# A hybrid convolution decoder layer: the token-row loads go out from SP's DMA queue in place of GpSimd's

## Chip, cores and metric

One Trainium2 chip, all 8 cores. Each core runs the same program on its own share of the tokens, and no core talks to another. The time is that of the slowest core in device microseconds, as the median of several executions.

## What is computed

The layer takes a prompt of 8 x 2048 tokens and 128 x 8 sample tokens, all 1024 wide. Each core gets one prompt sequence and 16 sample sequences of 8 tokens: 2176 token rows. Cut to what matters here:

```
u    = rmsnorm(h, g_mix);  proj = u @ w_in                      # 1024 -> 9 * 1024
ya   = (a_b * dwconv3(a_c * a_h) * silu(a_z)) @ w_out_a         # short convolution
yb   = (silu(layernorm(dwconv31(b_v * sigmoid(b_g)) + bias)) * silu(b_z)) @ w_out_b
m    = sigmoid(gate_a) * ya + sigmoid(gate_b) * yb
h    = h + m @ w_o
h    = h + sigmoid(rmsnorm(h, g_ple) @ w_pg) * (p @ w_pe)
y    = rmsnorm(h, g_final)
```

## The kernel before

A core's 2176 rows are done in two blocks, one after the other: block 0 with 1152 rows (9 tiles of 128), block 1 with 1024 (8 tiles). Each block goes through the same stages. Stages 2 to 5 work with channels on the partitions: projections (`mm8`, L581), the two convolutions, the layer norm, the gated output projections. Their weights come through a ring of 14 tiles, loaded from GpSimd's queue (L393) as TensorE frees them. The last part of stage 5 is the loop over `BORDER`, eight calls of `s5_b`, in which the weights of the next stage are fetched too: `wpg_stage` (L515) loads rows of `w_pg` from SP's queue, `wpg_scale` (L519) scales them on ScalarE.

Stage 6 then goes through the block's tiles with tokens on the partitions. For tile t:

- `s6_A` (L1000): 16 matmuls, m @ w_o. `s6_Aev` (L1011, VectorE) adds the token rows `xs`, ScalarE copies the sum as bf16 into `xb` (L1015), and SP issues a DMA transpose of `xb` into `u2T` (L1019). The first and the last tile are transposed on TensorE instead (`s6_B`, L1028, copied by L1032).
- `s6_C`: 4 matmuls with `pT` (L1044), then 16 with `u2T` (L1052), then a tanh on ScalarE (L1066).
- `s6_E` and `s6_D` (L1074, L1089, VectorE) join the two and scale by the final norm; SP stores the tile to `y` (L1093).

TensorE takes A(t+1) before C(t), and `u2T` of tile t+1 is asked for right after A(t+1) is evicted, so a transpose has about the time of C(t) and of A(t+2) and the `pT` matmuls to land.

While block 0 is in stage 6, the first steps of block 1 are done beside it: for each of block 1's 8 tiles ScalarE squares the token rows (`s1_stats`), VectorE scales them into `xn` (`s1_scale`, L544), and SP issues a DMA transpose into `uT` (`s1_xbar`, L550). So each step of stage 6 of block 0 reads two tiles of x: its own one again, for the residual, and one of the next block. In block 1 there is only the own one.

These 25 reads of x share four buffers `xs0` to `xs3`, in the order of the list `XU` (n0, n1, o0, o1, n2, o2, n3, o3, ...: n of the next block, o of the own one). `xload` (L455) issues one read of 512 KB, `xdone` asks for the next as soon as a buffer is free, that is, after the VectorE instruction that read it last. The first four reads are asked for in the `BORDER` loop of block 0, one in each of its last four rounds (`xload(i - 3)`, L1249). All 25 are issued by GpSimd, in its program order, between the ring loads and the small steps of the row norms (L416, L421).

The first nine tiles of x, at the kernel's start, are loaded apart from that by `x0load` (L483) from SP's queue; the ninth takes buffer `xs0` again and signals on a semaphore of its own, `x0e`.

`Sched` makes a list of all operations in the order of the Python program. An engine takes its own ones in this order and waits before each until what it depends on is done. A wait therefore holds up everything behind it on that engine. SP's order for one step t of stage 6 in block 0 is: transpose u2T(t+1), store y(t-1), transpose uT(t+1).

Of the kernel before, what the change touches and what calls it, by code (L numbers as in the profile page):

```python
# [167 lines left out]
def build_program():  # L168
    nc = bass.Bass("TRN2", target_bir_lowering=False)

    def din(name, shape):
        return nc.dram_tensor(name, shape, F32, kind="ExternalInput").ap()
# [4 lines left out]
    x_d = din("x", [NTOK, D])  # L177
# [27 lines left out]
    with contextlib.ExitStack() as st:  # L205
        def sb(name, shape, dt):
            return st.enter_context(nc.sbuf_tensor("t_" + name, shape, dt))
# [38 lines left out]
        NXS = 4  # L246
        xs = [sb(f"xs{i}", [128, D], F32) for i in range(NXS)]
# [21 lines left out]
        S = Sched(nc)  # L269
# [165 lines left out]
        def tiles_of(b):  # L435
            blk = BLOCKS[b]
            n = (2 * NP // blk["pb"]) * blk["wb"] // 128
            return [blk["row0"] + 128 * i for i in range(n)]

        XU = []  # L440
# [9 lines left out]
        def xload(upto):  # L450
            while xst["nl"] < min(upto, len(XU)):
                u = xst["nl"]
                xst["nl"] += 1
                k = u % NXS
                S.add("pool", lambda e, k=k, r=XU[u]: e.dma_start(out=xs[k][:], in_=x_d[r:r + 128, :]),  # L455
                      writes=[f"xs{k}"], dma=f"xs{k}")

        def xuse(row0):
# [5 lines left out]
        def xdone(u):  # L464
            xst["done"].add(u)
            while xst["nd"] in xst["done"]:
                xst["nd"] += 1
            xload(xst["nd"] + NXS)
# [4 lines left out]
        x0 = []  # L473
        xw = [t.rearrange("p (h m) -> p h m", h=2) for t in xs]
        for i, r in enumerate(tiles_of(0)):
            t, nm = (xw[i], f"xs{i}") if i < NXS else (AB[i - NXS], ("A0", "A1", "B0", "B1")[i - NXS]) \
# [3 lines left out]
        def x0load(i):  # L480
            t, nm = x0[i]
            r = tiles_of(0)[i]
            S.add("sp", lambda e: e.dma_start(out=t, in_=x_d[r:r + 128, :].rearrange("t (h m) -> t h m", h=2)),  # L483
                  writes=[nm], dma=f"x0{nm}" if i < NXS + 4 else "x0e")

        x0load(0)
        S.add("sp", lambda e: e.dma_start(out=vecs[:], in_=vecs_d), writes=["vecs"], dma="vecs")
        for i in range(1, NXS + 4):
            x0load(i)
# [3 lines left out]
        for i in range(2):  # L493
# [6 lines left out]
              writes=["ssq63"])  # L500
# [62 lines left out]
        def do_block(bi, blk):  # L563
# [577 lines left out]
            if bi == 0:  # L1141
# [18 lines left out]
                pump(1)  # L1160
                sc(0)
                x0load(NXS + 4)
                fill(20)
                turn(0, 4)
# [82 lines left out]
            for i, j in enumerate(BORDER):  # L1247
                s5_b(j)
                if bi == 0 and i >= 4:  # L1249
                    xload(i - 3)  # L1250
                if i == 0:
                    wpg_stage(0)
                    wpg_stage(1)
                    if nxt:
                        S.add("sp", lambda e: e.dma_start(out=gmix, in_=gmix_d), writes=["gmix"], dma="gmix")
                if bi == 1 and i == 2:
                    S.add("sp", lambda e: e.dma_start(
                        out=hist_d[:, 0:480], in_=sb_d.rearrange("c s w -> c (s w)")), dma="hist")
                if i == 6 and nxt:
                    s1_scale(*s1_stats(nxt[0]), 0)  # L1260
                if i == 7 and nxt:
                    pre[1] = s1_stats(nxt[1])
                if 2 <= i <= 5:
                    for k in (2 * i - 4, 2 * i - 3):
                        wpg_scale(k)
                        if k + 2 < NCH:
                            wpg_stage(k + 2)
                if i == 5:
                    last_weights("wpe", [0, 1])
                if i == 5:  # L1270
                    S.add("pool", lambda e, r0=blk["row0"]: e.dma_start(
                        out=pT[:, :, 0:N], in_=pT_d[:, :, r0:r0 + N].rearrange("q p t -> p q t")),
                        writes=["pT"], dma="pT")
                    if last:

                        S.add("pool", lambda e: e.drain())
# [139 lines left out]
```

How the kernel before makes its waits and increments, by code:

```python
            def run(engname, e):  # L123
                waited = {}
                for o in ops:
                    if o["eng"] != engname:
                        continue
                    need = {}
                    for d in o["deps"]:
                        od = ops[d]
                        v = od["seq"] * (16 if od["dma"] is not None else 1)
                        if v > need.get(od["chan"], 0):
                            need[od["chan"]] = v
                    for c, v in need.items():
                        if waited.get(c, 0) >= v:
                            continue
                        e.wait_ge(sems[c], v)
                        waited[c] = v
                    ins = o["fn"](e)
                    if o["signal"]:
                        ins.then_inc(sems[o["chan"]], 16 if o["dma"] is not None else 1)
                if engname == final_wait_eng:
                    for c, v in final.items():
                        if waited.get(c, 0) < v:
                            e.wait_ge(sems[c], v)
```

## Time and profile before

| | |
|---|---|
| median of 3 runs | 886.32 us (882.65 to 887.99) |
| the profiled execution | 886.32 us |
| its span on the slowest core, core 3 | 884.6 us |
| spans of all cores | 863.0 to 884.6 us |
| TensorE busy in that span | 852.0 us, 96% |
| VectorE, ScalarE, GpSimd | 476.7, 305.9, 225.2 us |
| DMA queue 0 (GpSimd's) | 70.83 MB |
| DMA queue 1 (SP's) | 61.29 MB |

The profile shows one execution, on the core whose span was longest. Times in the rows are counted from that core's first instruction. PEclk is the granted TensorE clock as a share of 2.4 GHz. The DMA share is the mean busy share of 16 DMA engines as their packets' times add up, and it can exceed 1 where packets of two queues overlap on an engine. "Landing" is the time from the issue of a DMA to its semaphore.

### The profile page before, as it was taken

The page shows a single profiled execution, that of the slowest core. Times are in us where ns is not written, and L with a number is a line of the kernel's source. Part 1 is how long each engine was busy: PE and PEld are TensorE (multiplying, and loading weights), DVE is VectorE, ACT ScalarE, POOL GpSimd, SP SyncE. Part 2 cuts the span into 40 slices and gives each one's busy share as a digit, 9 for nine tenths or more (in the row PEclk, how much of TensorE's full clock was granted, in tenths as well). Part 3 has the DMA queues.
Part 4 walks back from the last instruction along what each step waited for, and adds up shares of the span by engine and source line. Part 5 has one row for each costly group of instructions (what it writes and reads, how often), then busy time and mean ns, then how long its engine had stood idle before and what let it go on. Part 6 is the DMA issues. An engine that isn't in the chain of part 4 may idle for free.

```text
span 884.6 us, 16617 instructions; the slowest of 8 cores (863.0 to 884.6 us)
## 1 busy us (share of the span) xinstructions
PE 852.0 (96%) x5790; PEld 501.6 (57%) x5790; DVE 476.7 (54%) x672; ACT 305.9 (35%) x430; POOL 225.2 (25%) x427
## 2 busy tenths in 40 slices
PE   8899999999999999999869999999999999999995
PEld 3677777777777777773324444444444444444442
DVE  4545566776848622344646344555567374234565
ACT  4212232232345522435635212222224343142554
POOL 4432333333112211133533222222221121000221
PEclk9999999999999999999989999999999999999998
DMA  8999999999959754997997698999998798342542
GB/s 237 154 173 195 211 159 159 168 159 168 159 105 183 112 86 67 203 169 194 199 194 222 134 164 122 138 136 154 141 138 123 177 197 128 51 150 41 148 114 103
DMA packets 88825, 133.43 MB, mean 151 GB/s; under 512 B 37272, under 2 KB 45736, under 8 KB 86696
## 3 DMA queue, kind: packets, MB, share of 16 engines
q0 software_dynamic: 36992, 70.83, 48.9%
q1 hardware_dynamic: 51608, 61.29, 34.3%
q8 instruction: 47, 0.77, 0.4%
q14 instruction: 34, 0.28, 0.1%
q10 hardware_dynamic: 144, 0.26, 0.1%
HBM read 169.26 MB, written 17.25 MB: 211 GB/s over the span
## 4 chain that ended last, share of the span: by engine, by line
PE 83%; DMA 7%; DVE 3%; issue 2%; ACT 2%; SPq 1%; POOL 0%; DVEq 0%; POOLq 0%; ACTq 0%
PE ps L581 70%; DMA t_xs<-x 5%; PE ps L1052 5%; PE ps L1000 4%; PE ps L719 3%; DMA t_u2T<-t_xb 2%; PE ps L1044 1%; ACT t_tmp L413 1%; SPq L483 1%; DVE t_cbuf L1011 1%; DVE t_tmp L860 0%; SPq L490 0%; DVE t_uT L558 0%; ACT t_xb L1015 0%; DVE t_tmp L863 0%
## 5 line engine op out<-in xcount | busy, mean ns | idle before, releaser
L581 PE MATMUL ps<-t_uT,t_ring 128*128 128x288 bf16 (+1 forms) x3456 | 545.1, 319 | 2.8 <-DVE t_uT L558 2.4
L581 PEld LDWEIGHTS ps<-t_uT,t_ring 128*128 128x128 bf16 x3456 | 338.0, 98 | 202.7 <-issue 15.7
L393 POOL DMA_DIRECT2D t_ring<-w_in x144 | 78.5, 546 | 302.9 <-PE ps L581 281.0
L1052 PE MATMUL ps<-t_reg,t_u2T 128*128 128x512 bf16 x272 | 66.1, 399 | 13.5 <-DMA t_u2T<-t_xb 11.5
L937 ACT ACTIVATE t_tmp<-ps 128x576 f32<-128x576 f32 (+1 forms) x48 | 36.7, 772 | 113.6 <-PE ps L581 113.6
L945 DVE SCALAR_TENSOR_TENSOR t_tmp<-t_tmp,ps 128x576 f32<-128x576 f32 (+1 forms) x27 | 24.6, 910 | 85.8 <-PE ps L581 85.8
L581 PE MATMUL ps<-t_yaT,t_ring 128*128 128x288 bf16 (+1 forms) x384 | 63.9, 325 | 0.0
L581 PE MATMUL ps<-t_cbuf,t_ring 128*128 128x288 bf16 (+1 forms) x384 | 61.6, 317 | 0.0
L1000 PE MATMUL ps<-t_cbuf,t_yaT 128*128 128x512 bf16 x272 | 61.6, 381 | 0.0
L1052 PEld LDWEIGHTS ps<-t_reg,t_u2T 128*128 128x128 bf16 x272 | 27.2, 102 | 50.8 <-issue 23.1
L904 DVE TENSOR_TENSOR t_tmp<-ps,t_tmp 128x576 f32<-128x576 f32 (+1 forms) x24 | 21.8, 912 | 60.1 <-PE ps L581 60.1
L643 DVE SCALAR_TENSOR_TENSOR t_vta<-t_tmp,ps 128x512 bf16<-128x512 f32 (+1 forms) x24 | 20.7, 863 | 60.4 <-ACT t_tmp L640 52.9
L413 ACT ACTIVATE t_tmp<-t_cbuf 128x1024 bf16<-128x1024 f32 x37 | 38.8, 1050 | 39.4 <-DVE t_cbuf L1077 33.1
L581 PEld LDWEIGHTS ps<-t_yaT,t_ring 128*128 128x128 bf16 x384 | 38.2, 100 | 22.9 <-issue 3.4
L640 ACT ACTIVATE t_tmp<-ps 128x576 f32<-128x576 f32 (+1 forms) x24 | 18.6, 775 | 91.5 <-PE ps L581 91.5
L581 PEld LDWEIGHTS ps<-t_cbuf,t_ring 128*128 128x128 bf16 x384 | 37.6, 98 | 21.4
L1000 PEld LDWEIGHTS ps<-t_cbuf,t_yaT 128*128 128x128 bf16 x272 | 26.6, 98 | 32.2 <-issue 1.2
L416 POOL TENSOR_SCALAR t_msq<-t_ssq 128x1 f32<-128x1 f32 x50 | 14.1, 283 | 115.0 <-ACT t_tmp L413 114.7
L902 ACT ACTIVATE t_tmp<-ps 128x576 f32<-128x576 f32 (+1 forms) x24 | 18.6, 775 | 69.5 <-PE ps L581 69.5
L1074 DVE SCALAR_TENSOR_TENSOR t_cbuf<-t_cbuf,ps 128x1024 f32<-128x1024 f32 x16 | 19.5, 1220 | 39.5 <-ACT t_cbuf L1066 39.5
L890 ACT ACTIVATE t_tmp<-ps 128x576 f32<-128x576 f32 (+1 forms) x24 | 18.6, 775 | 58.9 <-PE ps L581 53.2
L421 POOL TENSOR_TENSOR t_rsd<-t_msq,t_mhalf 128x1 f32<-128x1 f32 x50 | 32.0, 641 | 7.7 <-POOL t_msq L416 0.4
(115 smaller groups left out, 815.4 us busy)
## 6 DMA issues: line engine op xcount, KB each, us to landing
t_ring<-w_in POOLq DMA_DIRECT2D x144, 256.0 KB, 6.8
t_xs<-x POOLq DMA_DIRECT2D x25, 512.0 KB, 7.9
y<-t_cbuf SPq DMA_DIRECT2D x16, 512.0 KB, 4.3
t_reg<-vd SPq DMA_DIRECT2D x32, 132.0 KB, 6.0
t_reg<-vd SPq DMA_DIRECT2D x32, 131.9 KB, 6.4
t_reg<-vd SPq DMA_DIRECT2D x32, 131.9 KB, 7.5
t_reg<-vd SPq DMA_DIRECT2D x32, 131.9 KB, 8.2
t_ring<-w_cv POOLq DMA_DIRECT2D x16, 256.0 KB, 9.1
```

The lines of the kernel that those rows point to most:

```text
L393: S.add("pool", lambda e, k=k, src=src: e.dma_start(out=ring[k][:, :], in_=src), writes=[f"ring{k}"], dma=f"ring{k}")
L413: S.add("act", lambda e, c=c: e.activation(out=junk.rearrange("p (h m) -> p h m", h=2), in_=src_ap, func=AF.Square, accum_out=ssq[:, c:c + ...
L421: S.add("pool", lambda e, c=c: e.tensor_tensor(out=rsd[:, c:c + 1], in0=msq[:, c:c + 1], in1=mhalf[:, 0:1], op=ALU.pow), reads=[f"msq{c}", ...
L581: S.add("pe", lambda e, k=k, si=si, c0=c0: e.matmul(ps[:, b + si, 0:wb], lhsT=ring[k_][:, 128 * k:128 * k + 128], rhs=src[:, k, c0:c0 + wb ...
L643: S.add("dve", lambda e, bv=bv, tg=tg, u=u: e.scalar_tensor_tensor(out=pph(vt[v], u), in0=pcols(two(tg)), scalar=1.0, in1=pcols(pp(bv)), o ...
L719: S.add("pe", lambda e, b=b, r=r, i=i, g=g, wc=wc, rhs=src[:, c0:c0 + w], w=w: e.matmul(ps[32 * g:32 * g + 32, b + r, 0:w], lhsT=ring[kc][ ...
L904: S.add("dve", lambda e: e.tensor_tensor(out=two(tz), in0=pp(bb), in1=two(tz), op=ALU.mult), reads=pres(bb) + [tzr], writes=[tzr])
L937: S.add("act", lambda e: e.activation(out=two(tg), in_=pp(bg), func=AF.Tanh, scale=0.5), reads=pres(bg), writes=[tgr])
L945: S.add("dve", lambda e: e.scalar_tensor_tensor(out=dst.rearrange("p (s n) -> p s n", s=2), in0=two(tg), scalar=1.0, in1=pp(b), op0=ALU.ad ...
L1000: S.add("pe", lambda e, h=h, k=k: e.matmul(ps[:, b + h, :], lhsT=yaT[:, k, 128 * ti:128 * ti + 128], rhs=wo_t[:, k, 512 * h:512 * h + 512] ...
L1052: S.add("pe", lambda e, h=h, k=k: e.matmul(ps[:, bg + h, :], lhsT=u2Ts[sl][:, k, :], rhs=wpg_t[:, k, 512 * h:512 * h + 512], start=(k == 0 ...
L1074: S.add("dve", lambda e: e.scalar_tensor_tensor(out=B2, in0=B2, scalar=1.0, in1=ps[:, be:be + 2, :], op0=ALU.add, op1=ALU.mult), reads=pre ...
```

## The change

The reads of x by `xload` are issued by SP in place of GpSimd, all 25 of them, at the same places of the program. The ninth tile of the start, which was on SP already, signals on the semaphore of buffer `xs0` in place of one of its own. Sizes, buffers and the conditions under which a read may go out stay as they are.

```diff
@@ -452,7 +452,7 @@
                 u = xst["nl"]
                 xst["nl"] += 1
                 k = u % NXS
-                S.add("pool", lambda e, k=k, r=XU[u]: e.dma_start(out=xs[k][:], in_=x_d[r:r + 128, :]),
+                S.add("sp", lambda e, k=k, r=XU[u]: e.dma_start(out=xs[k][:], in_=x_d[r:r + 128, :]),
                       writes=[f"xs{k}"], dma=f"xs{k}")
@@ -481,7 +481,7 @@
             S.add("sp", lambda e: e.dma_start(out=t, in_=x_d[r:r + 128, :].rearrange("t (h m) -> t h m", h=2)),
-                  writes=[nm], dma=f"x0{nm}" if i < NXS + 4 else "x0e")
+                  writes=[nm], dma=f"x0{nm}" if i < NXS + 4 else "xs0")
```

SP's order for one step t of stage 6 in block 0 becomes: u2T(t+1), y(t-1), x, x, uT(t+1); in block 1: x, u2T(t+1), y(t-1).

## Rows read from the trace of the kernel before

**Rows 1.** Spans and mean granted clock of two of the eight cores.

```profile
core 3: 884.6 us, clock 0.982
core 6: 863.0 us, clock 0.997
```

**Rows 2.** Windows, core 3: busy PE, PEld, DVE, ACT, POOL; PEclk, DMA share, GB/s.

```profile
395.00:487.00 92.00, 77.72 (x345) 33.73 (x343) 50.18 (x44) 46.35 (x71) 34.05 (x63) 0.94 0.98 202
820.00:840.00 20.00, 20.00 (x95) 9.04 (x94) 10.61 (x9) 11.17 (x16) 5.23 (x13) 1.00 0.54 134
844.00:860.00 16.00, 16.00 (x76) 7.21 (x74) 10.06 (x9) 9.12 (x14) 3.09 (x9) 1.00 0.35 99
```

**Rows 3.** Windows, core 6, the same columns: its stage 6 of block 0.

```profile
391.00:469.00 78.00, 72.81 (x345) 32.46 (x344) 50.37 (x44) 46.58 (x71) 37.80 (x65) 1.00 1.08 234
```

**Rows 4.** Timeline of PE, core 3: start, us; in brackets idle before and releaser.

```profile
395.25 7.07 PE L1000 MATMUL ps<-t_cbuf,t_yaT 128*128 128x512 bf16 x32
...
406.10 5.05 PE L1052 MATMUL ps<-t_reg,t_u2T 128*128 128x512 bf16 x16
...
445.74 5.30 PE L1052 MATMUL ps<-t_reg,t_u2T 128*128 128x512 bf16 x16 [4.54 <-DMA t_u2T<-t_xb]
...
460.68 5.07 PE L1052 MATMUL ps<-t_reg,t_u2T 128*128 128x512 bf16 x16 [5.33 <-DMA t_u2T<-t_xb]
...
483.48 3.61 PE L1052 MATMUL ps<-t_reg,t_u2T 128*128 128x512 bf16 x16 [0.87 <-ACT t_u2T L1032]
486.93 3.40 PE L581 MATMUL ps<-t_uT,t_ring 128*128 128x512 bf16 x15
```

**Rows 5.** Waits, core 3, 395 to 487 us: total, times, longest.

```profile
PE ps L1052 <- DMA t_u2T<-t_xb: 11.5, 3, 5.3
```

**Rows 6.** Chain that ended last, core 3: start, us, what.

```profile
388.64 12.70 DMA t_xs<-x
401.43 0.70 DVE t_cbuf L1011
...
429.68 12.35 DMA t_xs<-x
...
444.62 15.79 DMA t_u2T<-t_xb
...
842.31 3.45 PE ps L1052 x16
...
850.08 3.45 PE ps L1052 x16
```

**Rows 7.** Timeline of POOL, core 3, 387 to 430 us.

```profile
388.12 0.53 POOL L393 DMA_DIRECT2D t_ring<-w_in  x1 [3.30 <-PE ps L581]
...
420.85 1.13 POOL L455 DMA_DIRECT2D t_xs<-x  x2
```

**Rows 8.** Timeline of SP, core 3: start of issue, us it took.

```profile
371.22 0.33 SPq L515 DMA_DIRECT2D t_xb<-w_pg  x1
...
419.99 0.66 SPq L1093 DMA_DIRECT2D y<-t_cbuf  x1
420.75 1.83 SPq L550 DMA_TRANSPOSE t_uT<-t_xn  x1
426.11 1.29 SPq L1019 DMA_TRANSPOSE t_u2T<-t_xb  x1
...
450.76 8.17 SPq L550 DMA_TRANSPOSE t_uT<-t_xn  x1
...
844.48 1.23 SPq L1019 DMA_TRANSPOSE t_u2T<-t_xb  x1
```

**Rows 9.** Landing of u2T (L1019), core 3: 400 to 480, then 840 to 870 us.

```profile
DMA to landing us min/median/max: 3.1/7.0/15.8
DMA to landing us min/median/max: 3.1/3.1/3.1
```

**Rows 10.** Landing of the x reads (L455), core 3, 400 to 480 us.

```profile
DMA to landing us min/median/max: 5.5/9.0/14.7
```

## The prediction

> **What bounds the kernel now.** I read the spans first, then the windows, then TensorE's timeline in the window that stands out, then the chain behind its waits, and last the two queues and their landings. The spans of the cores, which run the same program, lie over 20 us apart [rows 1]; something that is not in the program decides the time. The windows say where: in stage 6 of block 0 TensorE of core 3 is busy 77.72 of 92 us, so 14.3 us idle, and its mean clock is 0.94 [rows 2]; core 6 has the same stage done in 78 us with 5.2 us idle at clock 1.00 [rows 3]. In stage 6 of block 1 TensorE is busy without a break, 20.00 of 20.00 us [rows 2]. There a step takes 7.77 us, from one L1052 group at 842.31 to the next at 850.08 [rows 6]. Nine such steps are 69.9 us; the stage took 486.93 - 395.25 = 91.7 us on core 3 [rows 4]. About 2.3 us of the difference belong to the first and last tile, which are transposed on TensorE (an estimate: 0.87 us of wait at the last one [rows 4], the same at the first, and the matmuls of it), so some 19.5 us are lost, in this one stage of this one core.
>
 The chain shows what stood before those waits: a read of x that landed after 12.70 us and let the first eviction start at 401.43, another that took 12.35 us, then a transpose u2T of 15.79 us [rows 6]. When nothing else is in flight u2T lands in 3.1 us; here the median is 7.0 [rows 9] and that of the x reads 9.0 [rows 10].
>
> Is the DMA simply full? The share times the window gives DMA time. From 844 to 860 us each step has one u2T and one y store: 0.35 x 16 us over 16 / 7.77 = 2.06 steps, 2.7 us a step. From 820 to 840 us one x read is added: 0.54 x 20 over 2.57 steps, 4.2 us, so an x read is worth 1.5 us. A step of stage 6 in block 0 has y, two transposes and two reads: 2.7 + 1.35 (uT taken as half of 2.7) + 3.0 = 7.0 us, under 7.77. But its share is 0.98 x 92 / 9 = 10.0 us a step [rows 2]. So the same transfers cost 3 us more per step when reads on GpSimd's queue and transposes on SP's are in flight together. I read that as queues that hold each other up on the engines; it is an inference, since no run separates them yet.
>
> **The change, part by part.**
>
> GpSimd loses 25 issues; a pair takes 1.13 us [rows 7]. It is busy 34 of the 92 us [rows 2], so the time is hidden under its own idle time: worth 0. Without that cover the row norms would come some 0.6 us earlier, and still nothing waits.
>
> SP gains the 25. The nearest issue on SP, a 512 KB read too, takes 0.33 us [rows 8]. A step then holds SP for 1.3 (u2T) + 0.7 (y) + 0.7 (pair) + 1.8 (uT) = 4.5 of 7.77 us. The pair waits for the `s1_scale` that frees a buffer; behind it stands uT, which waits for the same instruction, so nothing ready is held up. The 0.7 us fall on uT, which nobody needs until block 1's first projection at 486.93. In block 1 the read waits for the eviction and stands before u2T, which waits for ScalarE's copy of that same eviction. Worth 0, bound 0.7 us a step if it did reach u2T. The ninth starting tile's semaphore changes no order: its next use is 350 us later. Worth 0.
>
> The first reads come earlier. On GpSimd they stand behind ring loads that wait for TensorE (388.12 after 3.30 idle [rows 7]), and the third, the first tile's residual, goes out at 388.64. On SP they stand behind the last `w_pg` row, issued at 371.22 [rows 8], with free buffers: out by about 372.5. Even with the longest landing seen, 14.7 us [rows 10], that is there at 387. The first eviction then waits for its matmuls only, half of 7.07 us after 395.25 [rows 4]: 398.8 in place of 401.43. TensorE finishes A(1) at 402.3, 7.07 us after 395.25, does the transposes and the `pT` matmuls (some 1.7 us, an estimate), and starts the first L1052 group near 404 in place of 406.10; without the gaps in front I give it 3.6 us, not 5.05. It ends at 407.7 in place of 411.15: 3.4 us. Bounds: 0, if the earlier reads only push ring loads back (the ring is 14 deep, hence not my value), and 4.
>
> One queue in place of two. The order on SP's queue becomes u2T, y, x, x, uT. The next u2T was issued 5.4 us after uT, 426.11 - 420.75, and y just before at 419.99 [rows 8]. In front of it are 1.35 + 3.0 + 1.35 = 5.7 us of work. With a start of 1.7 us (3.1 less 1.35 of movement) that is through at 427.4; u2T then lands near 429, about 3 us after its issue. It may take 5.6 us: issued at 844.48 [rows 8], needed at 850.08 [rows 6]. So 2.5 us are to spare, and x, asked for one step ahead of its first reader, has landed by then. If so, the 11.5 us of waits go, and with them the slow groups behind two of them, 1.85 + 1.6 us: 15.0 us. That the crowding leaves nothing behind I don't believe: I keep half of core 6's idle time, 2.6 us, and take 12.4. The bounds are 15.0 and a loss that the last rival prices.
>
> The Trainium skill speaks against this term: "DMA: Bandwidth & Descriptors", section "Issuing engines are not separate DMA queues", says that DMAs started by different engines run on the same 16 engines and interleave, and that spreading them over issuers saves only issue time. By it the queue would be worth nothing, and the sum would hold the 3.4 us alone, 882.9. The trace agrees that they share the engines (landings stretch when both are in flight) and leaves open whether sharing one queue costs less.
>
> Sum for core 3: 884.6 - 3.4 - 12.4 = 868.8 us of span. The execution's time, 886.32, is 1.7 us over its span and is the median of the three runs itself: 870.5. I take core 3 as the slowest still; a core whose stage is good already gains only the first term.
>
> **Rivals.**
>
> The crowding stays (0.23). Each step still has two reads, a store and two transposes in flight, in one order or another; if the transposes stall because of the company and not because of the queue, only the early reads pay. For it: even the best core spends 1.08 x 78 / 9 = 9.4 us of DMA time a step [rows 3]. Against it: the sum of the parts is 7.0. Time: 886.3 - 3.4 = 882.9.
>
> One queue is slower (0.14). A read in front holds the transpose, and SP is held at a transpose's issue when its queue is behind (8.17 us once [rows 8]), which now holds the reads too. If the 10.0 us of DMA time per step are work and not overlap, one queue in order needs them in full: nine steps of 10.0 us, with 2.3 for the ends 92.3, and about seven of them with a group at the lower clock, 1.6 each: 103.5 in place of 91.7, the first tile's gap left out already. That is 884.6 + 11.8 + 1.7 = 898. It is slower than before once a step needs over 8.7 us: 9 x 8.7 + 2.3 + 11.2 = 91.8.
>
> The change does nothing at all is no case of its own: at the least the early reads move, and this is in the first rival.
>
> **How the numbers follow.** The forecast, most of the crowding gone, has 0.63, with 870.5 and its own range of 865 to 877: the whole 19.5 us gone gives 866.8, and half of the 12.4 gone 876.7. The first rival lies at 880 to 888, the second at 891 to 900. About 1%, 9 us, is what a measurement of this kernel can tell from no change. So faster by over 1% has 0.63, within 1% 0.23 and slower 0.14. The range that should hold the time takes in the forecast and the first rival: 865 to 890.
>
> **What would show it.** Right: x on SP in the timeline at about 372 us, the first eviction of stage 6 before 399.5, u2T landing under 5.6 us in nearly all steps, the DMA share per step between 7 and 8 us, TensorE over 95% busy in that stage, and spans of the cores closer than 10 us. Wrong in the queue term: u2T's median still near 7 with waits of TensorE for it. Wrong in sign: SP held for several us at transposes while the x reads behind them go out late, and ScalarE or VectorE waiting for x. What would make it wrong is that transposes stall for another reason than the second queue.

## The result, and the profile after

The changed kernel takes 870.63 us (median; 869.63 to 871.44) beside 884.79 us for the kernel before (882.65 to 887.99) on the same chip: a ratio of 0.9836, 95% interval 0.980 to 0.9873. The forecast was 870.5 us, range 865 to 890. On a second chip, in the experiments below, the same pair gave 864.35 us, just below that range, beside 881.41 us for the kernel before, ratio 0.984 (0.9732 to 0.9948).

In the profiled execution core 2 is the slowest now. Two cores, span and mean granted clock, against [rows 1]:

```profile
core 2: 868.1 us, clock 0.986
core 5: 857.4 us, clock 0.996
```

The spread over the cores went from 21.6 us to 10.7 us. The windows of core 2, its stage 6 of block 0 and a stretch of block 1's (the columns of [rows 2]: busy PE, PEld, DVE, ACT, POOL; PEclk, DMA share, GB/s):

```profile
393.80:468.80 75.00, 73.76 (x334) 33.04 (x340) 50.19 (x44) 46.16 (x71) 28.29 (x47) 0.95 1.04 230
820.00:840.00 20.00, 19.89 (x93) 9.01 (x93) 12.88 (x11) 11.06 (x16) 3.71 (x10) 1.00 0.52 145
```

TensorE is idle for 1.2 of 75.0 us in the stage, where core 3 was idle for 14.3 of 92 [rows 2] and core 6, the best one, for 5.2 of 78 [rows 3]. The timeline of its matmuls (start, us, line; in brackets idle before and releaser), against [rows 4]:

```profile
393.81 6.85 PE L1000 MATMUL ps<-t_cbuf,t_yaT 128*128 128x512 bf16 x31
...
401.84 3.61 PE L1052 MATMUL ps<-t_reg,t_u2T 128*128 128x512 bf16 x15
...
409.61 3.62 PE L1052 MATMUL ps<-t_reg,t_u2T 128*128 128x512 bf16 x16
...
442.96 4.38 PE L1052 MATMUL ps<-t_reg,t_u2T 128*128 128x512 bf16 x16
...
465.34 3.61 PE L1052 MATMUL ps<-t_reg,t_u2T 128*128 128x512 bf16 x16 [0.87 <-ACT t_u2T L1032]
...
468.79 2.32 PE L581 MATMUL ps<-t_uT,t_ring 128*128 128x512 bf16 x10
```

The first L1052 group starts 8.0 us after the stage does, not 10.9, and the next one 7.77 us later: a step without a gap. No wait for `u2T`'s transpose is left on this core; the 0.87 us at 465.34 are the last tile, which TensorE transposes itself. Some groups in the middle of the stage take 4.2 to 4.4 us, as the one at 442.96. There the granted clock was 0.81 to 0.85 (413 to 418, 430 to 434 and 443 to 447 us; 0.95 in the mean of the stage), on an engine that had been busy nearly all the time; nothing is waited for there. The waits of the same core and stretch (total, times, longest), against [rows 5]:

```profile
DVE t_cbuf L1011 <- DMA t_xs<-x: 2.2, 1, 2.2
PE ps L1052 <- ACT t_u2T L1032: 0.9, 1, 0.9
```

SP's queue on core 2 (start, time of the issues), against [rows 7, 8]:

```profile
370.06 20.74 SPq L455 DMA_DIRECT2D t_xs<-x  x4
...
421.50 1.28 SPq L1019 DMA_TRANSPOSE t_u2T<-t_xb  x1
422.88 0.72 SPq L1093 DMA_DIRECT2D y<-t_cbuf  x1
423.79 1.55 SPq L455 DMA_DIRECT2D t_xs<-x  x2
425.39 1.26 SPq L550 DMA_TRANSPOSE t_uT<-t_xn  x1
```

One read went out at 361.81 and three more between 370.06 and 372.81; the last of the group of four, the fifth read, waited for a free buffer until 390.47. The issues of this step take 4.8 us together, where 4.5 were estimated. The landings of `u2T` and, below, of the x reads on core 2 from 398 us to the end of the stage, against [rows 9, 10]:

```profile
DMA to landing us min/median/max: 3.1/4.2/4.9
DMA to landing us min/median/max: 4.9/6.2/7.6
```

On core 3 in [rows 9] `u2T` took up to 15.8 us; over all eight cores the longest was 19.8 us (core 5) and is now 9.2 us (core 0).

For the comparisons below one measure is used: the length of stage 6 of block 0, from the first L1000 to the first L581 of block 1 in each core's TensorE timeline. Everything around it stays nearly constant: the stage starts at 390 to 398 us in the kernels compared, block 1 takes 320.6 us up to its stage 6 (up to 325.2 on cores 0 to 3 of the first chip, before and after), and the last stage 73.5 to 74.6. It is read from the one profiled execution of each kernel; for e2b and e3b that was the slowest of its group (870.38 and 876.80 us), so their stages come out a little long. The ratios are estimates to the kernel before, run on the same chip beside each, and differ a little from the quotient of two medians.

| kernel | time, us | before on that chip, us | ratio to before, 95% | stage 6 of block 0, mean of 8 cores / longest, us |
|---|---|---|---|---|
| before | 884.79 | | | 84.1 / 95.8 |
| after | 870.63 | 884.79 | 0.9836 (0.980 to 0.9873) | 74.3 / 77.2 |
| after, second chip (a0) | 864.35 | 881.41 | 0.984 (0.9732 to 0.9948) | 73.3 / 76.3 |
| early reads only (e1b) | 878.89 | 881.41 | 0.9964 (0.991 to 1.0018) | 80.5 / 92.5 |
| pairs only (e2b) | 866.10 | 884.08 | 0.978 (0.9741 to 0.9819) | 75.1 / 77.3 |
| pairs from ScalarE (e3b) | 873.66 | 884.08 | 0.9881 (0.9842 to 0.992) | 80.9 / 86.1 |
| before, stores left out (e5) | 866.59 | 881.41 | 0.9851 (0.9751 to 0.9951) | 75.4 / 77.2 |
| after, stores doubled (e6) | 871.02 | 881.41 | 0.9902 (0.9868 to 0.9936) | 79.9 / 84.9 |

The times in this table are medians of the executions in which neither half of the chip ran longer at a lower granted clock; in the first group of runs (e1, e2, e3, e4) cores 0 to 3 did so with every kernel, so only cores 4 to 7 are read there.

### The profile page after: what moved, and what is told of

Read it like the earlier page. It is cut to its first block, busy times and chain, and to the rows that moved or that the text cites. A ratio compares the mean times of both kernels' runs of the same rounds, so it can differ in the third digit from the quotient of the medians.

```text
span 868.1 us, 16566 instructions; the slowest of 8 cores (857.4 to 868.1 us)
## 1 busy us (share of the span) xinstructions
PE 844.2 (97%) x5746; PEld 500.3 (58%) x5790; DVE 476.8 (55%) x672; ACT 306.3 (35%) x430; POOL 215.1 (25%) x402
## 4 chain that ended last, share of the span: by engine, by line
PE 90%; DMA 5%; issue 2%; ACT 2%; DVE 1%; SPq 1%; POOLq 0%; ACTq 0%; DVEq 0%; POOL 0%
PE ps L581 71%; PE ps L1000 7%; PE ps L1052 7%; PE ps L719 3%; DMA t_xs<-x 3%; PE ps L1044 2%; DMA t_reg<-vsd 1%; ACT t_tmp L737 1%; DMA vd<-t_vta 1%; SPq L686 0%; DVE t_uT L558 0%; ACT t_tmp L413 0%; SPq L693 0%; PE ps L781 0%; PE ps L1028 0%
## 5 line engine op out<-in xcount | busy, mean ns | idle before, releaser
L581 PE MATMUL ps<-t_uT,t_ring 128*128 128x288 bf16 (+1 forms) x3429 | 541.3, 318 | 6.7 <-DVE t_uT L558 2.4
L581 PEld LDWEIGHTS ps<-t_uT,t_ring 128*128 128x128 bf16 x3456 | 337.1, 98 | 204.2 <-issue 21.3
L945 DVE SCALAR_TENSOR_TENSOR t_tmp<-t_tmp,ps 128x576 f32<-128x576 f32 (+1 forms) x27 | 24.6, 910 | 86.1 <-PE ps L581 86.1
L1052 PE MATMUL ps<-t_reg,t_u2T 128*128 128x512 bf16 x267 | 62.6, 385 | 2.2 <-ACT t_u2T L1032 2.0
L581 PE MATMUL ps<-t_yaT,t_ring 128*128 128x288 bf16 (+1 forms) x383 | 62.8, 321 | 0.1
L1000 PE MATMUL ps<-t_cbuf,t_yaT 128*128 128x512 bf16 x267 | 62.3, 386 | 0.3
L581 PE MATMUL ps<-t_cbuf,t_ring 128*128 128x288 bf16 (+1 forms) x382 | 61.5, 317 | 0.1
L581 PEld LDWEIGHTS ps<-t_yaT,t_ring 128*128 128x128 bf16 x384 | 37.9, 99 | 22.4 <-issue 3.4
L581 PEld LDWEIGHTS ps<-t_cbuf,t_ring 128*128 128x128 bf16 x384 | 37.6, 98 | 21.4
L1052 PEld LDWEIGHTS ps<-t_reg,t_u2T 128*128 128x128 bf16 x272 | 26.7, 99 | 35.7 <-issue 7.8
L1000 PEld LDWEIGHTS ps<-t_cbuf,t_yaT 128*128 128x128 bf16 x272 | 26.9, 99 | 33.3 <-issue 5.5
L421 POOL TENSOR_TENSOR t_rsd<-t_msq,t_mhalf 128x1 f32<-128x1 f32 x50 | 34.6, 691 | 8.0 <-POOL t_msq L416 0.9
L737 ACT ACTIVATE t_tmp<-ps,t_vecs 128x512 f32<-128x512 f32 (+1 forms) x24 | 15.7, 654 | 53.1 <-PE ps L719 47.7
```

Of the source, the lines that this page charges most:

```text
L421: S.add("pool", lambda e, c=c: e.tensor_tensor(out=rsd[:, c:c + 1], in0=msq[:, c:c + 1], in1=mhalf[:, 0:1], op=ALU.pow), reads=[f"msq{c}", ...
L581: S.add("pe", lambda e, k=k, si=si, c0=c0: e.matmul(ps[:, b + si, 0:wb], lhsT=ring[k_][:, 128 * k:128 * k + 128], rhs=src[:, k, c0:c0 + wb ...
L737: S.add("act", lambda e, out=out, cols=cols: e.activation(out=cols(ph(te)), in_=out[0], func=AF.Identity, scale=vcol(V_MA), bias=vcol(V_BC ...
L945: S.add("dve", lambda e: e.scalar_tensor_tensor(out=dst.rearrange("p (s n) -> p s n", s=2), in0=two(tg), scalar=1.0, in1=pp(b), op0=ALU.ad ...
L1000: S.add("pe", lambda e, h=h, k=k: e.matmul(ps[:, b + h, :], lhsT=yaT[:, k, 128 * ti:128 * ti + 128], rhs=wo_t[:, k, 512 * h:512 * h + 512] ...
L1052: S.add("pe", lambda e, h=h, k=k: e.matmul(ps[:, bg + h, :], lhsT=u2Ts[sl][:, k, :], rhs=wpg_t[:, k, 512 * h:512 * h + 512], start=(k == 0 ...
```

## Experiments

### The two parts apart

Theory: both terms of the sum are real, some 3.4 us from the early reads and 12.4 from the one queue. Rival: the early reads alone pay. "Early" are the first five of the 25 reads, "pairs" the rest.

```diff
-                S.add("pool", ... x_d[r:r + 128, :] ...)
+                S.add("sp" if u < 5 else "pool", ...)      # e1, e1b: early only
+                S.add("pool" if u < 5 else "sp", ...)      # e2, e2b: pairs only
```

> The first five reads of x (those asked for in the BORDER loop of block 0) go out from SP, the other twenty from GpSimd as before. Crowding of two queues (the forecast's main term): only the first tile's gap goes, 3.4 us, so about 881 us, with TensorE still waiting for u2T and u2T's median landing near 7 us in stage 6 of block 0. Rival, the early reads are the whole effect: about 871 us.

> The reverse: the first five reads from GpSimd as before, the other twenty from SP. Crowding of two queues: about 874 us (870.6 plus the first tile's 3.4 us), u2T landing under 5.6 us. Rival, the early reads are the whole effect: about 885 us.

Measured on cores 4 to 7: with the early reads alone spans of 863.3 to 879.0 us, as uneven as before; with the pairs alone 865.4 to 869.0. The two were run again on other chips, the early reads together with the changed kernel itself:

> The changed kernel itself, beside the others of this call: 869 to 872 us where the chip grants the clock of the first comparison; stage 6 of block 0 in 72 to 77 us on each core of an undisturbed die.

> As the first run of this kernel (the first five reads from SP, twenty from GpSimd), to have it in one call with the changed kernel. If the crowding is the main term: 8 to 12 us over the changed kernel. If the early reads are: within 4 us of it.

> The first five reads from GpSimd, the other twenty from SP, a second time beside a chip with its full clock. If the pairs are the main term: 866 to 872 us, no u2T landing over 8 us. If the early reads carry it: 880 us and more.

The times are in the table. Early only: 2.5 us less than its 881.41, with an interval that includes no change. Spans of two of its cores:

```profile
core 4: 857.8 us, clock 0.996
core 7: 878.1 us, clock 0.988
```

Core 4 is as good as any core after the change, core 7 is not. Core 7's chain in that stage (start, us, what):

```profile
399.38 3.48 PE ps L1052 x16
...
425.25 5.42 DMA t_u2T<-t_xb
...
443.44 9.25 SPq L550
...
452.88 18.53 DMA t_u2T<-t_xb
...
471.55 6.54 PE ps L1052 x16
```

The first tile is as early as the early reads make it (399.38). From there the landings of `u2T` grow: 3.6, 3.1, 4.9, 5.4, 6.4, 13.7 and 18.5 us, tile by tile. Ahead of the seventh SP itself is held for 9.25 us at the issue of `uT`, and behind that wait TensorE's group takes 6.54 us in place of 3.48, at a granted clock of 0.54, close to the lower of its two levels. What was won at the front is lost behind.

Pairs only: 866.10 us, the whole gain within what can be measured. Two waits of its slowest core, core 1, in the stage (total, times, longest):

```profile
DVE t_cbuf L1011 <- DMA t_xs<-x: 3.8, 1, 3.8
PE ps L1052 <- DMA t_u2T<-t_xb: 0.4, 1, 0.4
```

And the landing of `u2T` on that core:

```profile
DMA to landing us min/median/max: 3.1/4.2/5.4
```

The late first read is still there, 3.8 us of VectorE's waiting, but no transpose runs away (7.4 us at most on any core). From the stage's start to the first L1052 group it takes 10.1 us in the mean of the cores (10.2 before) and 8.2 in the changed kernel (a0). So the early reads do give each core 1.9 us, as the means of the stage say too (75.1 and 73.3 us), and the time, 866.10 and 864.35 on two chips, cannot resolve it.

### Does the place in the queue matter?

Theory: the place decides little, as long as all is in one queue. Rival: it pays that the reads go out ahead of `uT`. The pair is asked for after `uT` here.

```diff
-            xdone(k)
+            held.append(k)
...
+            while held:
+                xdone(held.pop(0))
```

The second half stands in `s1_xbar`, after the transpose.

> All 25 reads from SP, but the pair of a step goes out after uT in place of before it, so that the next u2T has the pair directly in front of it. If one queue is what counts: 869 to 873 us. If the order in the queue counts (u2T must find the queue empty): u2T lands over 5.6 us, TensorE waits for it, 876 to 885 us.

SP's queue on core 6, one step (this kernel's lines are 2 to 4 higher):

```profile
421.05 1.24 SPq L1023 DMA_TRANSPOSE t_u2T<-t_xb  x1
422.38 0.57 SPq L1097 DMA_DIRECT2D y<-t_cbuf  x1
423.32 2.99 SPq L552 DMA_TRANSPOSE t_uT<-t_xn  x1
426.41 1.02 SPq L455 DMA_DIRECT2D t_xs<-x  x2
```

The landing of `u2T` on the same core, over the stage:

```profile
DMA to landing us min/median/max: 3.1/4.2/7.1
```

Spans of cores 4 to 7 are 862.7 to 866.2 us and their stages 73.3 to 76.2, as with the pairs in front. TensorE waits 0.5 to 3.0 us for `u2T` on these cores. The place between the transposes is not what pays.

### Which queue?

Theory: what hurts is a second queue beside the transposes. Rival: it is GpSimd's way of issuing alone, and ScalarE's queue would do as well as SP's. First five reads on SP, the rest on ScalarE.

```diff
-                S.add("sp", ...)
+                S.add("act" if u >= 5 else "sp", ...)
```

> The first five reads from SP, the other twenty from ScalarE's queue: a hardware queue, but not the one of the transposes. If any second queue beside the transposes crowds them: 878 to 885 us, DMA share near 10 us a step, u2T's median landing near 7 us. If it is GpSimd's software queue alone that crowds: 870 to 874 us, u2T under 5.6 us. ScalarE's own waits for VectorE may add up to 1 us a step, which shows as idle time of ScalarE, not as landings.

Cores 4 to 7 have spans of 880.1 to 883.4 us, a loss to SP's 865 to 869. But core 6's waits say why this does not answer the question (total, times, longest):

```profile
ACT t_cbuf L1066 <- POOL t_rsd L421: 11.2, 4, 2.9
PE ps L1044 <- ACT t_cbuf L1066: 6.2, 5, 2.4
```

The first row is put down to GpSimd; ScalarE's timeline shows what stood there. The two reads go out at 430.83 us, when VectorE's `s1_scale` has freed their buffer, and the tanh only behind them, after 2.88 us of idle time:

```profile
430.83 1.30 ACTq L455 DMA_DIRECT2D t_xs<-x  x2
432.35 1.11 ACT L1066 ACTIVATE t_cbuf<-ps,t_rsd 128x1024 f32<-128x1024 f32 x1 [2.88 <-POOL t_rsd L421]
```

A read that waits for its buffer holds ScalarE's own work behind it, and that held TensorE. So the reads were moved behind the step's tanh, when their buffers are free:

```diff
-            xdone(k)
+            held.append(k)
...
+                while held:
+                    xdone(held.pop(0))
```

The first half stands in `s1_scale` and in `s6_Aev`, the second after `s6_C` of the step (one more `xdone` is called in the `BORDER` loop).

> The first five reads from SP, the other twenty from ScalarE's hardware queue, asked for after the tanh of the step, when the instruction that frees the buffer is done, so that ScalarE isn't held (about the moment at which GpSimd sent them before). If any second queue beside the transposes makes landings run away on some cores: u2T up to 10 us and more on some core, idle times over 10 us there, 876 to 882 us. If it takes GpSimd's software queue: no landing over 8 us, 866 to 871 us.

873.66 us: between SP's 866.10 and the 878.89 with GpSimd. Core 0 of it, TensorE's wait for `u2T` in the stage (its L1054 is the others' L1052):

```profile
PE ps L1054 <- DMA t_u2T<-t_xb: 10.9, 2, 8.3
```

The longest piece of the chain behind it (start, us, what):

```profile
455.99 13.53 DMA t_u2T<-t_xb
```

So a landing past 13 us occurs with ScalarE's queue too, once; on the other seven cores the longest are 7.4 to 10.1 us. The mean of the stage is 80.9 us, like 80.5 with GpSimd's (e1b), the longest 86.1 in place of 92.5, but in the slowest of four executions. By the medians the twenty reads cost 7.6 us on ScalarE's queue against e2b on the same chip, or 9.3 against a0 on another, where on GpSimd's they cost 14.5 (e1b against a0). So a second queue beside the transposes loses about half of the gain when it is ScalarE's and most of it when it is GpSimd's, which has the worse outliers too. These reads are also asked for later than the others'. In e4 a later place cost nothing; but on core 5 of e3b VectorE waits 7.2 us in all for x, where 2.9 us are the most on any core of a0. How much of ScalarE's loss is lateness was not tried by itself.

### The transfers alone

Only the DMAs of a step, 16 steps in a row for each arrangement, nothing of the layer computed: two transposes and a store from SP, two x reads from the queue named.

```diff
+        PHASES = ["pool", "sp", "act", None, "pool", "sp", "act"]      # m1; the last three without transposes
+        PHASES = ["act", "sp", "pool", "sp", "pool", "act", "sp"]      # m2; all with transposes
```

> No layer is computed: the kernel only moves what one step of stage 6 of block 0 moves (two DMA transposes of 256 KB and one store of 512 KB from SP, two reads of x of 512 KB), 16 steps in a row, each waiting for what was sent two steps earlier. Seven stretches: reads from GpSimd, from SP, from ScalarE, no reads; then without the transposes reads from GpSimd, SP, ScalarE. Crowding of two queues: 9 to 10 us a step with reads from GpSimd and from ScalarE, about 7 from SP; without transposes all three alike, 4 to 5 us. If only the software queue crowds: ScalarE's stretch is like SP's. If the DMA engines are full whatever the queue: the first three stretches alike, within 0.5 us a step.

> The transfers of a step alone, again 16 steps to a stretch, all with transposes, in another order: reads from ScalarE, SP, GpSimd, SP, GpSimd, ScalarE, SP. If the queue sets the cost: every SP stretch at 7.5 to 7.8 us a step on all cores, GpSimd's at 7.8 to 9.2 with the cores apart, ScalarE's between. If the order of the stretches made the difference: the two stretches of one engine differ by more than SP from GpSimd.

VectorE's mark at the end of a stretch, core 3, m1: its first five, of GpSimd's queue, SP's, ScalarE's, of no reads, and of GpSimd's without transposes (start, us, line; in brackets the time waited and for what):

```profile
128.56 0.06 DVE L527 MEMSET t_cbuf<- 1x1 f32 x1 [120.95 <-DMA t_uT<-t_xn]
251.72 0.06 DVE L527 MEMSET t_cbuf<- 1x1 f32 x1 [123.11 <-DMA t_uT<-t_xn]
371.73 0.06 DVE L527 MEMSET t_cbuf<- 1x1 f32 x1 [119.95 <-DMA t_uT<-t_xn]
442.42 0.06 DVE L527 MEMSET t_cbuf<- 1x1 f32 x1 [70.62 <-DMA t_uT<-t_xn]
521.22 0.06 DVE L527 MEMSET t_cbuf<- 1x1 f32 x1 [78.74 <-DMA scr<-t_cbuf]
```

The same marks in m2, core 3, its second to fourth stretch, of SP's queue, GpSimd's and SP's again:

```profile
250.53 0.06 DVE L527 MEMSET t_cbuf<- 1x1 f32 x1 [121.03 <-DMA t_uT<-t_xn]
402.52 0.06 DVE L527 MEMSET t_cbuf<- 1x1 f32 x1 [151.92 <-DMA t_uT<-t_xn]
528.27 0.06 DVE L527 MEMSET t_cbuf<- 1x1 f32 x1 [125.70 <-DMA t_uT<-t_xn]
```

A stretch over 16 is a step. The first stretch of each kernel is counted from the issue of its first read (2.2 us in m1, 1.1 in m2); its first transpose goes out only at 8 to 11 us, so its figure is up to 0.5 us a step too long. On core 3 GpSimd's stretch of m1 gives (128.56 - 2.2) / 16 = 7.9 us, SP's (251.72 - 128.56) / 16 = 7.7; in m2 GpSimd's gives (402.52 - 250.53) / 16 = 9.5 and SP's behind it 7.9. Over all cores and both kernels:

| x reads from | us a step, lowest to highest over the cores | means of the stretches |
|---|---|---|
| SP | 7.5 to 7.9 | 7.66, 7.56, 7.71, 7.67 |
| ScalarE | 7.2 to 8.3 | 7.71, 7.71 (a first stretch), 7.87 |
| GpSimd | 7.6 to 9.5 | 8.60 (a first stretch), 8.36, 8.29 |
| none | 4.2 to 4.4 | |
| any of the three, no transposes | 4.8 to 5.2 | |

TensorE wants a step every 7.77 us. SP's queue alone supplies one in just under that in the mean, GpSimd's and SP's together in more. Without transposes the three queues are alike, so GpSimd's reads are not slow as such. ScalarE's are hardly slower here than SP's (7.7 to 7.9 beside 7.6 to 7.7). That is what was expected if only GpSimd's queue crowds, and not the 9 to 10 us of the theory; so the transfers alone speak for the rival, while e3b speaks in part against it, and its landing of 13.5 us stays without an explanation. In these kernels reads on GpSimd and ScalarE wait for a transpose of two steps back, those on SP only for their buffers, so their figures are upper bounds.

### More and less load

If a step on two queues needs just over 7.77 us, taking some 1.7 us of transfers out of it must stop the growth with the queues left as they were; putting as much into a step on the one queue must bring the loss back.

```diff
+                if bi == 1 or ti >= nt - 2:      # e5: before, stores of block 0's tiles 0 to 6 left out
                     S.add("sp", ... y_d[row0:row0 + 128, :] ...)
```

> The kernel before, reads on GpSimd's queue, with the stores of block 0's tiles 0 to 6 left out (those rows of y are missing). Backlog (a step brings 7.8 to 9.2 us of transfers on two queues against 7.77 us of matmuls, and what is over adds up): without the store a step brings 6.4 to 7.8 us, so u2T lands within 5.6 us on every core, TensorE idles under 5 us in stage 6 of block 0, the stage takes 74 to 79 us, the kernel 872 to 876 us. Rival, transposes stall whenever reads of another queue are in flight: landings of 10 us and more and idle times of 10 us and more stay on some cores, 880 to 885 us.

```diff
+                if bi == 0:                      # e6: after, and each tile of block 0 stored a second time
+                    S.add("sp", ... scr_d[ti, :, :] ... in_=Bbuf[sl])
```

> The changed kernel, with each tile of block 0 stored a second time to a scratch tensor, from SP. Backlog: a step brings 7.65 + 1.3 = about 9 us on one queue, over 7.77; u2T's landing grows from step to step past 5.6 us, the stage takes 83 to 92 us, the kernel 880 to 890 us. Rival, one queue keeps the transposes from stalling whatever it carries: the stage stays at 72 to 77 us, the kernel at 870 to 873 us.

Landing of `u2T` on core 3 with the stores left out:

```profile
DMA to landing us min/median/max: 3.1/3.4/4.3
```

The same with the stores doubled:

```profile
DMA to landing us min/median/max: 3.1/6.1/7.6
```

And two waits of that core in the stage with the stores doubled (total, times, longest; lines one higher there):

```profile
PE ps L1053 <- DMA t_u2T<-t_xb: 7.5, 4, 2.8
DVE t_cbuf L1012 <- DMA t_xs<-x: 3.0, 2, 2.4
```

With less load two queues do as well as one: 866.59 us, under the 872 to 876 expected, the longest landing over all cores 5.9 us. It is a store that was taken out; taking out another transfer was not tried. With more load on the one queue 6.7 us are lost in the time and 6.6 in the stage's mean, on every core (77.2 to 84.9 us), in many waits of at most 3.3 us; no landing is over 8.3 us. That is less than the backlog theory forecast: the stage stays under 83 us in the mean and the time under 880, and on core 3 the landings do not grow from step to step (3.9, 3.1, 6.5, 7.6, 6.2, 5.4 and 6.1 us). The rival's 72 to 77 us for the stage is missed as well. On two queues a similar mean (80.5 in e1b) comes with cores at 72.5 and at 92.5 us. So neither more load on one queue nor two queues with less load brought the run-away of some cores; it took both here. What makes the one queue degrade evenly is not settled by these runs.

## Why the prediction was right, step by step

- **The place.** Right: the stage named lost what was lost, and stage 6 of block 1 did not move.
- **Early reads, 3.4 us.** Right in the mechanism and for core 3: its first L1052 group starts 8.3 us after the stage's start in place of 10.9 and takes 3.61 us, 4.0 us together, the upper bound. As a term of the sum it does not add up: by itself 2.5 us with an interval that includes zero, behind the pairs 1.9 us in the mean of the cores and nothing that the time resolves. What it wins at the front can be lost behind, as on core 7 of e1b. The group behind the gap, like the two behind the long waits, ran at a granted clock of 0.68 to 0.71, a mix of the two levels and not the lower one alone.
- **One queue, 12.4 of 15.0 us.** Right: 14.5 us from e1b to a0 with the early reads in both, and 18.0 by the pairs alone. On core 3 itself the stage went from 91.7 to 75.2 us, which leaves 12.5 us beside the 4.0 of the early reads. That it meets the 12.4 so closely is luck: the 2.6 us that were kept stood for waits, but TensorE of core 3 is idle for only 0.9 us of the stage now, and what is left over is a granted clock of 0.95. For the pairs alone the upper bound was too low by 3 us: it counted three waits of core 3 and the slow groups behind two of them, while core 5 was idle for 19.5 us in the same stage; and the runs are of different chips.
- **A step of 7.0 us.** The term that was mis-sized. Measured: 7.65 on SP's queue. Without transposes three transfers of 512 KB take 5.0 us, so one is worth 1.67, where 1.5 (a read) and 1.35 (the store) were taken; the transposes are right, (4.3 - 1.67) / 2 = 1.3 us beside 1.35. The margin under 7.77 us is then 0.1 us and not 0.8, and 10 of 56 landings of `u2T` are past the 5.6 us allowed, up to 9.2. TensorE's waits for them stay short all the same, 0 to 3.1 us in all on each core.
- **Crowding, 3 us a step by the DMA share.** Too much. The share still makes 1.04 x 75 / 9 = 8.7 us a step after the change, beside 10.0 and 9.4 before, and not the 7 to 8 that I gave as a sign. Packets' times overlap in it (it exceeds 1). Timed by themselves two queues cost between 0 and 1.9 us a step more than one. The step was right in sign: 8.3 to 8.4 us against 7.77, though an upper bound, points to queues that fall behind.
- **SP's 25 issues, worth 0.** Right. A pair takes 1.5 us in place of 0.7, and in e4, with the pair behind `uT`, nothing was lost.
- **The sum.** 868.8 us of span were forecast for core 3, and 868.1 measured, but on core 2, and this is luck in part. Core 3 itself came out at 866.4: its stage began 3.2 us earlier and its block 1 took 1.4 us longer (325.1 us), and for neither had the sum a term. Core 2's span holds 4.6 us by which its block 1 is longer than on cores 4 to 7, at a granted clock of 0.99 with 1.3 us of waits (325.2 in place of 320.6 us). On the second chip all spans, 857.8 to 862.8 us, lie under the forecast. The gain is the fairer measure: 15.8 us forecast, 14.2 by the medians of the first chip and 17.1 by those of the second.
- **The rivals.** "The crowding stays" asked for 882.9 us and is ruled out by the pairs alone. "One queue is slower" was priced by 10.0 us of work a step from the share; the point from which it would decide, 8.7, was not reached at 7.65. e6 shows that a fuller single queue does cost, 6.6 us of the stage.
- **The Trainium skill's rule** ("DMA: Bandwidth & Descriptors", section "Issuing engines are not separate DMA queues"), that issuers share the same 16 engines and spreading DMAs over them saves only issue time: the first half agrees with the runs, the second does not where transposes are in the mix. e1b and a0 differ by 14.5 us, and in nothing but the queue of 20 reads; without transposes, 4.8 to 5.2 us for all three queues, it holds.
- **The signs.** x on SP by 372 us: seen, 361.81 to 372.81 on core 2. First eviction before 399.5: seen, 394.5 to 397.2 on all cores. `u2T` under 5.6 us in nearly all steps: 46 of 56. TensorE over 95% busy in the stage: 98% on core 2, 95 to 99% on the others. Cores closer than 10 us: 10.7, just missed, and 5.0 in a0. DMA share per step: missed.

## To carry to other kernels

Ask of a stage whether its transfers per step take less time than its matmuls per step, and time them by themselves: the busy share of the DMA engines does not say it (8.7 us by the share after the change, 7.65 timed alone). Where DMA transposes sit on the path, try to issue the ordinary transfers of the same stage from the transposes' own queue: here it paid 14.5 us against GpSimd's, and the two orders tried on the one queue were alike. Two edits that attack the same waiting should be priced as a pair, since the slowest core changes once one of them is in.

## What the hardware showed that I had not expected

- The same reads beside the same transposes cost 8.3 to 8.4 us a step (an upper bound) from GpSimd's queue and 7.6 to 7.7 from SP's, but 4.8 to 5.2 from any queue when no transposes are there.
- With two queues the landing of a transpose grows from tile to tile on some cores (3.6 to 18.5 us on core 7 of e1b) and not on others of the same execution (6.1 at most on core 4, span 857.8 us). Why these cores is open.
- A transpose's issue can hold SP for long: 1.2 us at 844.48 in [rows 8], 1.2 to 2.7 us in most steps of the changed kernel, 9.25 us in the chain of e1b, ahead of the landing of 18.5 us.
- ScalarE's queue is hardly slower than SP's when the transfers run alone (means of 7.7 to 7.9 us a step), and yet has a landing of 13.5 us inside the kernel. One candidate from the Trainium skill ("DMA: Bandwidth & Descriptors", section "Queues, rings and completion order") is that each DMA engine takes turns between queues packet by packet, so that reads on another queue pass a transpose that was issued before them. No run here separates that from other causes.
